# A trunk of two layers on one core: prologue in order of use, bias rows in small pieces, layers written out

## The reference

```python
h = rmsnorm(x, norm_mix[l])
proj = h @ w_in[l]          # queries, keys, values of mixers A and B, and an indexer
o_a = dsa_branch(...)       # 8 heads x 128, top 64 keys by the indexer, + relative bias
o_b = swa_branch(...)       # 16 heads x 64, window of two chunks of 64, sinks, + relative bias
g_a, g_b = split(sigmoid(h @ w_gate[l]))
x = x + (g_a * (o_a @ w_branch_a[l]) + g_b * (o_b @ w_branch_b[l])) @ w_out[l]
x = x + square(relu(rmsnorm(x, norm_mlp[l]) @ w_up[l])) @ w_down[l]
```

## Time and profile before

| | |
|---|---|
| Time, median of 3 runs | 2770.85 us (2769.07 to 2771.25) |
| The profiled execution's own time | 2771.44 us |
| its span in the trace | 2769.4 us |
| VectorE busy | 1563.2 us (56%) |
| ScalarE busy | 1262.6 us (46%) |
| GpSimd busy | 6.5 us |
| HBM read, written | 535 MB, 44 MB: 209 GB/s over the span |

### The profile page before, as it was taken

One profiled execution on the slowest core, in us unless ns is written; L12 is line 12 of the kernel. 1 busy time (PEld: TensorE's weight loads), 2 busy tenths in 40 slices (PEclk: granted clock), 3 DMA queues, 4 the chain that ended last, 5 costly groups with the idle time before them and its releaser, 6 DMA issues.

```text
span 2769.4 us, 34954 instructions
## 1 busy us (share of the span) xinstructions
PE 2716.8 (98%) x12042; PEld 2197.9 (79%) x12042; DVE 1563.2 (56%) x2158; ACT 1262.6 (46%) x1600; POOL 6.5 (0%) x16
## 2 busy tenths in 40 slices
PE   4999999999999999999999999999999999999997
PEld 4778878888888888888887887788888888888886
DVE  3475565556655555545656655555666555465555
ACT  2445554445443444434445455544444344343443
POOL 0000000000000000000000000000000000000000
PEclk7999999999999999999999999999999999999999
DMA  6765545667765756657766655466667566576675
GB/s 195 250 218 185 197 152 183 214 221 233 233 223 189 238 196 213 226 189 234 234 213 217 222 168 178 159 201 218 227 234 242 192 218 221 189 227 208 204 241 190
DMA packets 196807, 580.98 MB, mean 210 GB/s; under 512 B 21404, under 2 KB 64444, under 8 KB 196540
## 3 DMA queue, kind: packets, MB, share of 16 engines
q1 hardware_dynamic: 196668, 579.27, 64.1%
HBM read 535.15 MB, written 44.04 MB: 209 GB/s over the span
## 4 chain that ended last, share of the span: by engine, by line
issue 95%; DMA 2%; PE 2%; DVE 1%; SPq 0%; POOL 0%; ACT 0%; DVEq 0%; POOLq 0%; ACTq 0%
DMA raw<-in_w_main 1%; PE acc L380 1%; PE acc L382 1%; PE acc L381 1%; DMA bias_b<-bias_rows 0%; DMA raw<-in_w_misc 0%; DVE xs L1340 0%; DVE stage L1175 0%; DVE w_lo L924 0%; DMA scratch<-spread 0%; DVE h_hl L952 0%; ACT w_hi L630 0%; SPq L221 0%; SPq L253 0%; POOL bias_b L346 0%
## 5 line engine op out<-in xcount | busy, mean ns | idle before, releaser
L924 DVE TENSOR_TENSOR w_lo<-raw,w_hi 128x1024 fp32r<-128x1024 f32 (+1 forms) x944 | 1133.7, 1214 | 836.6 <-ACT w_hi L630 833.2
L630 ACT ACTIVATE w_hi<-raw 128x1024 fp32r<-128x1024 f32 (+1 forms) x944 | 989.6, 1053 | 1060.2 <-PE acc L382 993.1
L380 PE MATMUL acc<-w_hi,h_hl 128*128 128x512 f32 x2176 | 866.6, 398 | 28.8 <-DVE w_lo L924 28.8
L382 PE MATMUL acc<-w_hi,h_hl 128*128 128x512 f32 x2176 | 859.5, 395 | 0.0
L381 PE MATMUL acc<-w_lo,h_hl 128*128 128x512 f32 x2176 | 859.3, 395 | 0.0
L380 PE MATMUL acc<-w_hi,o_hl 128*128 128x512 f32 x1408 | 556.7, 395 | 0.0
L382 PE MATMUL acc<-w_hi,o_hl 128*128 128x512 f32 x1408 | 555.5, 395 | 0.0
L381 PE MATMUL acc<-w_lo,o_hl 128*128 128x512 f32 x1408 | 555.5, 395 | 0.0
L380 PEld LDWEIGHTS acc<-w_hi,h_hl 128*128 128x128 f32 x2176 | 410.6, 189 | 129.2 <-DVE w_lo L924 30.1
L382 PEld LDWEIGHTS acc<-w_hi,h_hl 128*128 128x128 f32 x2176 | 410.4, 189 | 96.0
L381 PEld LDWEIGHTS acc<-w_lo,h_hl 128*128 128x128 f32 x2176 | 410.8, 189 | 94.0
(11 more groups left out here) (136 smaller groups left out, 986.8 us busy)
## 6 DMA issues: line engine op xcount, KB each, us to landing
raw<-in_w_main SPq DMA_DIRECT2D x928, 512.0 KB, 4.2
scratch<-spread SPq DMA_DIRECT2D x70, 512.0 KB, 2.7
moved<-scratch SPq DMA_DIRECT2D x280, 128.0 KB, 3.5
raw<-in_w_misc SPq DMA_DIRECT2D x16, 336.0 KB, 3.7
bias_rows<-stage SPq DMA_DIRECT2D x1, 4608.0 KB
xs<-in_x SPq DMA_DIRECT2D x4, 512.0 KB, 6.2
out<-xs SPq DMA_DIRECT2D x4, 512.0 KB, 2.9
bias_b<-bias_rows SPq DMA_DIRECT2D x1, 1536.0 KB, 11.8
```

What stands on the lines that cost most here:

```text
L380: nc.tensor.matmul(o, a_hi, hi[:, kk], start=(k == 0), stop=False)
L382: last = nc.tensor.matmul(o, a_lo, hi[:, kk], start=False, stop=fin)
L630: nc.scalar.activation(w_hi[s][:, 0:2 * width], raw[r][:, 0:2 * width], ACT.Copy).then_inc(hi_ready, 1)
L924: nc.vector.tensor_tensor(w_lo[s][:, 0:2 * width], raw[r][:, 0:2 * width], w_hi[s][:, 0:2 * width].bitcast(F32), ALU.subtract).then_inc(lo ...
```

## The change

- SP loads in order of use: x block n, misc chunks 2n and 2n + 1, for n = 0 to 3, then main. ScalarE issues gains, table, one-hot and sinks.
- PE runs three matmuls of zeros (256 columns) at the start and three behind block 0's transposes. Block 1 is transposed ahead of misc chunk 0, block 2 behind chunk 1, block 3 behind chunk 3.
- ScalarE and VectorE do, for each block, its four pieces and then two splits. ScalarE takes over two of the four blocks' squares; a small copy stands first on it.
- The table's matmul stands behind main chunk 1 of unit 0, ScalarE's copy of it behind unit 0's chunk 6. VectorE's factors of the norm stand in the `take` of unit 0.
- The rows are stored 32 times each (1.18 MB), in four stores of 6 heads, behind chunks 0, 2, 4, 6 of unit 1. `bias_a` is loaded in four pieces of 32 partitions in unit 3, `bias_b` in four in unit 4.
- PE, ScalarE, VectorE and SP have the layers written out in place of loops. Behind the last layer x is no longer moved and split.

```diff
 LANDED = 16 * QUARTERS
-X3_TURNS, T_FIRST = 2, 6
+X3_TURNS, T_FIRST = 2, 8
+ROWS = A_HEADS + B_HEADS
+COPIES = 32
+BIAS_PIECES = P // COPIES
+WARM = 256
 JOBS = 16
...
-        first_turn = [acc[0][0], acc[0][1], acc[1][0], acc[1][1], turn, att[2]]
+        first_turn = [acc[0][0], acc[0][1], acc[1][0], acc[1][1], turn, att[2], acc[0][0], acc[0][1]]
+        rows = probs[1][0:ROWS, 0:REL]
+        hot = probs[0][0:N_BUCKETS, 0:REL]
...
-            def load_misc(l):
-                for c in range(N_MISC):
+            def load_misc(l, first, end):
+                for c in range(first, end):
...
+            def load_unit(l, at, chunks, passing=None, extra=None):
                 for c in range(chunks):
                     if c == 7 and passing:
                         passing[0]()
                     sp.wait_ge(lo_ready, at + (l * CHUNKS + c + 1))
                     sp.dma_start(raw[c % RAW][:], w_main[l, at + (c - N_MISC)]).then_inc(raw_in[c % RAW], 16)
+                    if extra and c % 2 == 0:
+                        extra(c // 2)
...
-            def load_bias():
-                sp.wait_ge(bias_stored, 16)
-                sp.dma_start(bias_a[:], bass.AP(bias_rows.tensor, P - 1, [[REL, P], [SKEW, A_HEADS], [1, SEQ]]))\
+            def store_rows(i):
+                heads = ROWS // 4
+                if i == 0:
+                    sp.wait_ge(rows_out, 1)
+                sp.dma_start(bass.AP(bias_rows.tensor, i * heads * SKEW, [[SKEW, heads], [REL + 1, COPIES], [1, REL]]),
+                             rows[i * heads:(i + 1) * heads].unsqueeze(1).to_broadcast([heads, COPIES, REL]))\
+                    .then_inc(bias_stored, 16)
+            def load_bias_a(i):
+                if i == 0:
+                    sp.wait_ge(bias_stored, 64)
+                sp.dma_start(bias_a[i * COPIES:(i + 1) * COPIES],
+                             bass.AP(bias_rows.tensor, P - 1 - i * COPIES, [[REL, COPIES], [SKEW, A_HEADS], [1, SEQ]]))\
                     .then_inc(bias_loaded, 16)
-                sp.dma_start(bias_b[:], bass.AP(bias_rows.tensor, P - 1 + SEQ - WINDOW_KEYS + A_HEADS * SKEW,
-                                                [[REL, P], [SKEW, B_HEADS], [1, WINDOW_KEYS]])).then_inc(bias_loaded, 16)
-            def load_layer(l, after_qi=None):
+            def load_bias_b(i):
...
+                             bass.AP(bias_rows.tensor, P - 1 - i * COPIES + SEQ - WINDOW_KEYS + A_HEADS * SKEW,
+                                     [[REL, COPIES], [SKEW, B_HEADS], [1, WINDOW_KEYS]])).then_inc(bias_loaded, 16)
+            def load_layer(l):
                 for u in range(N_WIN):
                     if u == 0:
                         passing = pass_on(l, E_MISC, pieces=2)
                     else:
                         passing = pass_on(l, E_QK + u - 1) if u <= 6 else pass_on(l, E_QB) if u == 9 else None
-                    load_unit(l, C_WIN + 8 * u, 8, passing)
-                    if u == 2 and after_qi:
-                        after_qi()
+                    extra = {1: store_rows, 3: load_bias_a, 4: load_bias_b}.get(u) if l == 0 else None
+                    load_unit(l, C_WIN + 8 * u, 8, passing, extra)
                 for n in range(NBLK):
...
-                    load_down(GROUPS - 1, n, pass_on(l, E_XD + n - 1) if n else None)
-            load_x(0)
-            sp.dma_start(gain[:], gains).then_inc(gain_in, 16)
-            sp.dma_start(tab[:, :], rel_bias).then_inc(tab_in, 16)
-            sp.dma_start(stage[0:N_BUCKETS, 0, 0:REL], onehot).then_inc(tab_in, 16)
-            for n in range(1, NBLK):
+                    load_down(GROUPS - 1, n, pass_on(l, E_XD + n - 1) if n and l < DEPTH - 1 else None)
+            for n in range(NBLK):
                 load_x(n)
-            sp.dma_start(nsink[:], sinks).then_inc(sinks_in, 16)
-            load_misc(0)
-            sp.wait_ge(rows_out, 1)
-            sp.dma_start(bass.AP(bias_rows.tensor, 0, [[SKEW, A_HEADS + B_HEADS], [REL + 1, P], [1, REL]]),
-                         stage[0:A_HEADS + B_HEADS, 1, 0:REL].unsqueeze(1).to_broadcast([A_HEADS + B_HEADS, P, REL]))\
-                .then_inc(bias_stored, 16)
-            load_layer(0, load_bias)
-            with sp.Fori(1, DEPTH) as l:
-                load_misc(l)
+                load_misc(0, 2 * n, 2 * n + 2)
...
-            pe.wait_ge(consts, 5)
-            for n in range(3):
+            def first_turns(n):
                 pe.wait_ge(x_in[n], 16)
                 for half in range(2):
-                    turn_into(first_turn[2 * n + half], n, half)
-                if n == 1:
-                    pe.wait_ge(tab_in, 32)
-                    pe.wait_ge(tab_neg, 1)
-                    pe.wait_ge(turn_took, 1)
-                    nc.tensor.matmul(acc[0][0][0:A_HEADS + B_HEADS, 0:REL], tab[:, :], stage[0:N_BUCKETS, 0, 0:REL],
-                                     start=True, stop=True).then_inc(rows_ready, 1)
-            pe.wait_ge(x_in[3], 16)
-            with pe.Fori(0, DEPTH) as l:
+                    k = 2 * n + half
+                    if k >= 6:
+                        pe.wait_ge(turn_took, k - 5)
+                    turn_into(first_turn[k], n, half)
+            def spread_rows():
+                pe.wait_ge(tab_in, 32)
+                pe.wait_ge(tab_neg, 1)
+                nc.tensor.matmul(turn[0:ROWS, 0:REL], tab[:, :], hot, start=True, stop=True).then_inc(rows_ready, 1)
+            def warm():
+                for i in range(3):
+                    nc.tensor.matmul(att[0][:, 0:WARM], moved[:, 0:P], moved[:, 0:WARM], start=True, stop=True)
+            pe.wait_ge(zeros, 1)
+            warm()
+            pe.wait_ge(consts, 5)
+            first_turns(0)
+            warm()
+            for l in range(DEPTH):
                 def took_of(e):
                     return l * TAKES + (e - E_M + NBLK + 1)
                 def misc_between(c):
-                    if c in (1, 3):
+                    if l == 0 and c in (1, 3):
+                        first_turns(c // 2 + 2)
+                    elif l and c in (1, 3):
                         half = c // 2
                         pe.wait_ge(dve_took, l * DVE_UNITS + 1)
-                        pe.wait_ge(turn_took, l * X3_TURNS + (T_FIRST + half))
+                        pe.wait_ge(turn_took, T_FIRST + (l - 1) * X3_TURNS + half)
                         turn_into(turn, 3, half)
                 unit(l * CHUNKS, N_MISC, h_lhs, att, misc_between, width=MISC,
-                     hold=[(c, turn_took, l * X3_TURNS + (c + 1)) for c in range(N_MISC)]
-                     + [(2 * n, moved_took, l * TAKES + (n + 2)) for n in range(3)])
+                     before=(lambda: first_turns(1)) if l == 0 else None,
+                     hold=[(c, turn_took, l * X3_TURNS + (c + 1)) for c in range(N_MISC) if l == 0 or c >= 6]
...
+                                         accum_out=squares[:, t, n:n + 1]).then_inc(sq_done, 1)
+            act.dma_start(gain[:], gains).then_inc(gain_in, 16)
+            act.dma_start(tab[:, :], rel_bias).then_inc(tab_in, 16)
+            act.dma_start(hot, onehot).then_inc(tab_in, 16)
+            act.dma_start(nsink[:], sinks).then_inc(sinks_in, 16)
+            act.wait_ge(zeros, 1)
+            nc.scalar.activation(sink_d[:], moved[:, 0:4], ACT.Copy)
             act.wait_ge(gain_in, 16)
-            for n in range(3):
+            for n in range(NBLK):
                 for half in range(2):
                     act.wait_ge(turned, 2 * n + half + 1)
                     first_hi(first_turn[2 * n + half], n, half, lambda k: gain[:, 0, k:k + 1])
-                if n < 2:
-                    split(0, n, MISC)
-            act.wait_ge(rows_ready, 1)
-            nc.scalar.activation(stage[0:A_HEADS + B_HEADS, 1, 0:REL], acc[0][0][0:A_HEADS + B_HEADS, 0:REL],
-                                 ACT.Copy)\
-                .then_inc(rows_out, 1)
-            split(0, 2, MISC)
-            with act.Fori(0, DEPTH) as l:
-                unit(l * CHUNKS, N_MISC, width=MISC, first=3,
-                     turns=lambda half: x3_hi(l, half))
+                split(0, 2 * n, MISC)
+                split(0, 2 * n + 1, MISC)
+                if n == 1:
...
+                def take_rows():
+                    act.wait_ge(rows_ready, 1)
+                    nc.scalar.activation(rows, turn[0:ROWS, 0:REL], ACT.Copy).then_inc(rows_out, 1)
                 def win_place(u):
                     if u == 0:
-                        return lambda: place(l, E_MISC, kiT_kbT[:], 2)
+                        def first_place():
+                            if l == 0:
+                                take_rows()
...
-                        taken = lambda: hi_moved_x(l, E_XD + n - 1, n - 1, bass.ds(l * 2 + 2, 1))
+                        if l < DEPTH - 1:
+                            taken = lambda: hi_moved_x(l, E_XD + n - 1, n - 1, 2 * l + 2)
```

(43 more changed lines are left out.)

57 lines of the change are left out of this document (32 added, 25 removed).

## The result

| | before | after |
|---|---|---|
| Time, median | 2771.05 us (4 runs, 2769.07 to 2771.67) | 2742.88 us (4 runs, 2741.51 to 2744.71) |
| Ratio | | 0.990 (95%: 0.988 to 0.992) |
| Profiled execution: time, span | 2771.44, 2769.4 us | 2744.71, 2743.0 us |
| Forecast | | 2733.5 (2729.5 to 2743) |

The change makes the kernel 28 us faster, where the prediction had 37.5. The time lies at the very end of the range. Some 9 us were gained and given back.

A forecast was written before the change was run, and what follows sets the result against it. It took PE, starved by weight loads queued behind the bias-row store, as the bound. From 2771.44 us: -34.7, -2.6, +0.7, -1.1, -0.6, +1.0 gave 2734.1, so a median of 2733.5 us, range 2729.5 to 2743.

The forecast's parts named there:

- main run starts earlier: PE's first main matmul moves from 62.7 to 28.0 us, the middle of 26.0 and 30.3: -34.7 us.
- no low level at its start: The main run's first matmuls no longer run at the 1.2 GHz spacing: -2.6 us.
- wait at the bias load: PE's 1.08 us wait at 133.77, behind bias loads in one lump, goes when they come in pieces: -1.1 us.
- layer switch: PE's 0.56 us idle between layers goes with no loop end there: -0.6 us, bounds 0 and -0.8.
- the bubble: Ahead of PE's main run, weight chunks wait behind the 4.72 MB bias-row store, some 31 us; PE waits 28.8 us on `w_lo`.
- the hidden steps on VectorE and ScalarE: Main chunks 0 to 3 are split in time for PE; chunk 3 at about 34 us against 34.4, no reserve at high end.
- step 2: New prologue up to the main run: start at 26.0 us with the clock high, 30.3 with it low; 28.0 taken.
- step 4: Bias stores in pieces in unit 1: delay inside a 7.2 us reserve; +1.0 us taken, ends 0 and 8.
- B: Rival: six-head pieces may get only six engines and starve PE 4.5 us; 2737 us, to 2742; chance 0.22.
- C: Rival: bubble remains in part, main chunks 0 to 3 late, a wait of 4 to 8 us; 2742 us; chance 0.12.
- hold by `rows_out`: SP waits for ScalarE's copy of the rows behind unit 1's first load: some 2 to 3 us late, inside the reserve.
- D: Rival: very few engines carry each piece; with one, 23 us a piece and 2797 us, slower; chance 0.03.

The follow-up runs named there:

- f1_nowarm: The kernel with four stores of 24 heads x 8 copies, without the six warm-up matmuls: 2734.14 us (4 runs).
- e1_24x8: The changed kernel with four stores of all 24 heads x 8 copies in place of 6 heads x 32: 2731.45 us, ratio to before 0.986.
- g2_one24x32: The changed kernel with one store of 24 heads x 32 copies behind chunk 0 of unit 1 in place of four: 2731.38 us (one run).
- g3_3x8heads: The changed kernel with three stores of 8 heads x 32 copies in place of four of 6 heads: 2738.80 us (one run).
- e2_unit2: The changed kernel with the bias traffic one unit later, stores still of 6 heads: 2741.01 us (4 runs).
- e4_before32: The kernel before with 32 copies instead of 128 in its one 24-head store, bias loaded in eight pieces behind unit 2: 2753.02 us, ratio 0.994.
- f4_lump: The kernel with stores of 24 heads x 8 copies, its eight bias loads issued in a row behind unit 2: 2737.73 us (one run).

## Why the prediction was right or wrong

The profiled executions, term by term; "measured" is from the two traces. "Low level" is TensorE's 1.2 GHz.

| term | predicted | measured |
|---|---|---|
| main run starts earlier | -34.7 | 62.70 to 27.13: -35.6 |
| no low level at its start | -2.6 | -2.6 |
| table matmul in the main run | +0.7 | 32.47 to 33.55 less one spacing: +0.85 |
| wait at the bias load | -1.1 | -1.1 |
| layer switch | -0.6 | -0.7 |
| what the stores in pieces add | +1.0 | 11.4 of waits and 2.0 of low level: +13.4 |
| sum | -37.3 | -25.8 |

The last matmul starts 26.3 us earlier, which the measured terms give but for 0.5 us; before and after:

```profile
2754.91 0.40 PE L382 MATMUL acc<-w_hi,o_hl 128*128 128x512 f32 x1
...
2728.64 0.40 PE L383 MATMUL acc<-w_hi,o_hl 128*128 128x512 f32 x1
```

**Right.** What bounded the kernel, the bubble and its size, the start of the main run (28.0 against 27.13), the hidden steps on VectorE and ScalarE (no wait for `w_lo` before 59 us, though main chunk 3 had no reserve on paper), the bias loads in pieces, the switch, and that the tail is untouched. The clock was at the high level from the first projection matmul, so the high end of step 2 was the true one, but for 1.1 us: it had the main run from 26.0 and x block 1 at 8.5, and PE got the block at 9.58. The 28.0 was the middle of two cases, neither of which came out there, and its nearness to 27.13 is partly luck. The rule on transposes of the Trainium skill (TensorE: Matmul & The Clock Gate, Part 4: PE-mode transpose) did not decide the start: the warm-ups did the work. f1_nowarm agrees with the rule, as its sixteen transposes from 5.37 on left the matmul at 11.04 at the 0.28 spacing.

**Wrong: step 4**, the term for the pieces, put at +1.0 with ends 0 and 8. It came to +13.4, beyond even its own end. That the time still lies in the range is due to the ends of rivals B and C. Three things failed in it.

First, the choice. I had both numbers in hand: that 24 heads kept 0.75 of the engines busy, and that six heads may get six. The rule of the Trainium skill (DMA: Bandwidth & Descriptors, Why a DMA increments its semaphore by 16 and not by 1) gave 12 and 6, and the trace had borne out the 12. For the six the changed kernel's trace agrees too, with 34.7% of 16 busy while only the store moved. So six was the likeliest case, not one of 0.22. I took the middle between "no stall" and "a small one" instead. e1_24x8 and g2_one24x32 show the step in its place: with 24 heads the term is 0.

Second, the size of a piece, in rival B too (2737, up to 2742). It had 7.0 us for a piece and two chunks; the stores came 8.1 us apart. (By B's own 309 GB/s two chunks are 3.4 us, not 3.2, and its sum 7.2.) The packet records, 115.5 us over six engines and four pieces, give 4.8 us for a piece, not 3.8. Four pieces then fall 10 us behind PE, not 5.6. And B forgot that a wait of 8.8 us lets the clock fall: 2.0 us more, though the same price stood in my sum for the first bubble, with the other sign.

Third, the path of the block's move. B counted it as bytes, 3.4 us at the full rate, and the forecast at nothing. But SP stands until the store of it has landed, and issues no chunk meanwhile; behind the fourth bias store that took 10.8 us. With the measured pieces and hold, B's sum is 10 + 3.4 + 0.8 less the reserve of 7.2, or 7.0 us of wait; the 4.4 us up to the 11.4 measured are near the 5.1 us estimated above for this standstill. That is worked out from the trace; no run took the move away.

The hold by `rows_out` was put at 2 to 3 us, inside the reserve. SP stood 0.76 us. e1_24x8 has the same hold and doesn't wait.

D, one engine to a piece, did not happen; C neither, as nothing waited for `w_lo` before 59 us.

## What to carry to other kernels

Before cutting a large store into pieces, ask over how many DMA engines each piece is spread: here stores of six heads loaded about six engines, and every full-width transfer behind them waited for these, while the view of all engines showed 61.5% busy. Cut along the other dimension (here copies, not heads), or not at all: the reserve of the raw buffers took one lump of 1.18 MB (g2_one24x32) and not four pieces that each put the loads 2.5 us behind. Look also for a point where the issuing engine stands until a transfer has landed, here the block's move: late transfers hurt most there. And where PE is 99% busy, a wait of more than a few us is to be priced with the low clock behind it: 1.5 to 2.5 us behind waits of 2.48 us (g3_3x8heads), 3.85, 4.31 and 8.80 us; behind the wait of 2.28 us there was none.

## What the runs showed of the hardware that I had not expected

- Issuing a store on SP took 0.31 us for the first piece of six heads and 2.9 to 3.6 us for the next ones, up to 4.3 us in e2_unit2; with 24 heads 0.35 to 0.91 us. I read it as SP standing in the issue itself while the engines are behind, so that the chunk loads behind it are late even in being issued; it isn't always so, as the third store of g3_3x8heads took 0.39 us.
- A store on fewer engines did not keep its rate per engine: 3.8 us a piece by the old store's rate, 4.8 by its packets. A packet of 1536 bytes took 109 ns in the old store, 150 in the six-head stores, 70 in e1_24x8, 92 in g2_one24x32.
- Eight loads of 32 partitions in a row held the chunks up more than two of 128 partitions with the same bytes: 4.31 and 3.85 us of wait (e4_before32, f4_lump) against 1.08. In e4_before32 SP needed 6.2 us to issue the eight (94.49 to 100.72), in the kernel before 1.1 us for the two (117.80 to 118.91). Spread behind every second chunk the eight cost PE no wait.
- With the warm-ups the clock rose at different points: in the profiled execution of the changed kernel the first transposes at 5.49 already ran at the high level (eight in 1.06 us), in e1_24x8 the second warm-ups still ran at the low one (2.77 us for six at 7.16, against 1.46). In both all projection matmuls were at the high level.
